# Expert weights loaded in units of 14 KB runs, one column step, two PSUM banks per token group

## The reference, cut to what matters

```python
def moe_swiglu(x, w_router, b_router, w1, w3, w2):
    logits = jnp.dot(t, w_router) + b_router                  # t: 256 x 1024
    top_val, top_idx = lax.top_k(logits, TOP_K)               # 2 of 8 experts
    top_w = jax.nn.softmax(top_val, axis=-1)
    gates = jnp.sum(jax.nn.one_hot(top_idx, N_EXPERTS) * top_w[..., None], axis=1)
    out = jnp.zeros_like(t)
    for e in range(N_EXPERTS):
        he = jax.nn.silu(t @ w1[e]) * (t @ w3[e])             # w1, w3: 1024 x 3584
        out = out + gates[:, e:e + 1] * (he @ w2[e])          # w2: 3584 x 1024
```

## Time and profile before

| | |
|---|---|
| median of 3 runs | 1250.5 us (1250.17 to 1252.01) |
| the profiled execution | 1252.75 us, span 1250.9 us |
| mean granted TensorE clock | 0.995 |
| busy: TensorE, its weight loads, VectorE, ScalarE, GpSimd | 1159.9, 664.2, 324.1, 261.7, 89.8 us |
| DMA | 114,767 packets, 421.65 MB, mean 337 GB/s; 98,256 packets under 8 KB |

### The profile page before, as it was taken

How to read it: one execution, slowest core, us unless ns; L and a number is a source line. 1 busy time by engine, 2 the same in 40 slices (tenths; PEclk the granted TensorE clock), 3 DMA queues, 4 the chain that set the end, 5 groups by cost and what they waited for, 6 DMA issues and landing times.

```text
span 1250.9 us, 28459 instructions
## 1 busy us (share of the span) xinstructions
PE 1159.9 (93%) x12516; PEld 664.2 (53%) x12517; DVE 324.1 (26%) x542; ACT 261.7 (21%) x394; POOL 89.8 (7%) x131
## 2 busy tenths in 40 slices
PE   8999999999999999999999877899987789998874
PEld 7888888888985346344346323334622332453232
DVE  6977766667974000000000000000000000000000
ACT  5885344335851000000000000000000000000000
POOL 4402200000001000100000100000010000001000
PEclk9999999999999999999999999999999999999998
DMA  7559565561498999999999999999999999999994
GB/s 237 191 178 323 190 199 183 187 202 68 153 364 319 362 373 419 405 399 409 421 404 410 407 405 410 410 421 400 409 407 404 404 409 418 399 404 409 419 401 150
DMA packets 114767, 421.65 MB, mean 337 GB/s; under 512 B 8722, under 2 KB 45199, under 8 KB 98256
## 3 DMA queue, kind: packets, MB, share of 16 engines
q1 hardware_dynamic: 109680, 413.18, 84.6%
q0 software_dynamic: 4960, 6.61, 2.2%
HBM read 416.54 MB, written 4.72 MB: 337 GB/s over the span
## 4 chain that ended last, share of the span: by engine, by line
PE 69%; DMA 23%; SPq 3%; DVE 2%; ACT 1%; issue 1%; POOL 0%; POOLq 0%; ACTq 0%; DVEq 0%
PE ps L1279 27%; PE ps L1304 13%; DMA w_raw<-in_moe_w_dram 11%; DMA w_hi_raw<-in_moe_w_dram 11%; PE ps L1010 7%; PE ps L727 5%; PE ps L729 5%; PE ps L728 5%; PE ps L1015 3%; SPq L544 3%; PE ps L1266 1%; DMA residual<-in_x_dram 0%; PE ps L1241 0%; PE ps L848 0%; PE ps L1257 0%
## 5 line engine op out<-in xcount | busy, mean ns | idle before, releaser
L1279 PE MATMUL ps<-w_raw,expert_in 128*32 128x512 f32 (+1 forms) x3416 | 342.1, 540 | 26.3 <-DMA w_raw<-in_moe_w_dram 25.3
L1279 PEld LDWEIGHTS ps<-w_raw,expert_in 128*32 128x32 f32 x3416 | 107.1, 110 | 244.3 <-issue 173.4
L1304 PE MATMUL ps<-w_raw,expert_hT 128*32 128x256 f32 x3040 | 174.1, 380 | 16.4 <-DMA w_raw<-in_moe_w_dram 16.4
L2333 DVE TENSOR_TENSOR expert_h<-expert_h,ps 128x1536 f32<-128x1536 f32 (+3 forms) x16 | 21.1, 1321 | 605.1 <-PE ps L1279 605.1
L1279 PE MATMUL ps<-w_hi_raw,expert_in 128*32 128x512 f32 (+1 forms) x1488 | 155.5, 548 | 13.9 <-DMA w_hi_raw<-in_moe_w_dram 13.9
L1304 PEld LDWEIGHTS ps<-w_raw,expert_hT 128*32 128x32 f32 x3040 | 95.8, 110 | 90.2 <-DMA w_raw<-in_moe_w_dram 24.0
L1770 DVE TENSOR_TENSOR w_lo<-w_raw,w_hi 128x2048 fp32r<-128x2048 f32 (+2 forms) x63 | 127.5, 2050 | 35.5 <-ACT w_hi L1346 35.4
L1010 PE MATMUL ps<-act_both,w_hi 128*128 128x512 f32 x352 | 122.4, 396 | 0.0
L1279 PEld LDWEIGHTS ps<-w_hi_raw,expert_in 128*32 128x32 f32 x1488 | 47.3, 111 | 111.0 <-issue 76.6
L1346 ACT ACTIVATE w_hi<-w_raw 128x2048 fp32r<-128x2048 f32 (+2 forms) x62 | 104.4, 1717 | 3.7 <-DMA w_raw<-in_mla_w_kvb_dram 2.1
L1015 PE MATMUL ps<-act_both,w_lo 128*128 128x256 f32 x352 | 91.3, 280 | 0.0
(11 more groups left out here) (365 smaller groups left out, 1105.7 us busy)
## 6 DMA issues: line engine op xcount, KB each, us to landing
w_raw<-in_moe_w_dram SPq DMA_DIRECT2D x160, 1024.0 KB, 18.9
w_hi_raw<-in_moe_w_dram SPq DMA_DIRECT2D x69, 1024.0 KB, 18.4
w_raw<-in_moe_w_dram SPq DMA_DIRECT2D x86, 768.0 KB, 22.8
w_raw<-in_ffn_w_dram SPq DMA_DIRECT2D x33, 1024.0 KB, 5.7
w_hi_raw<-in_moe_w_dram SPq DMA_DIRECT2D x36, 768.0 KB, 23.3
w_res_raw<-in_moe_w_dram SPq DMA_DIRECT2D x11, 1024.0 KB
w_raw<-in_lru_w_in_dram SPq DMA_DIRECT2D x8, 1024.0 KB, 5.4
w_res_raw<-in_moe_w_dram SPq DMA_DIRECT2D x6, 768.0 KB
```

Of the source, the lines that this page charges most:

```text
L1279: ins = pe.matmul(ps[j * STRIP:(j + 1) * STRIP, bank + g, 0:part], in_x[:, c, k, g * STRIP:(g + 1) * STRIP], w[:, j * part:(j + 1) * part] ...
L1304: ins = pe.matmul(ps[j * STRIP:(j + 1) * STRIP, bank, at:at + part], hT[t][:, a:a + STRIP], w[:, k * D + j * part:k * D + (j + 1) * part], ...
L2333: dve.tensor_tensor(h, h, regions(3, many, part), ALU.mult).then_inc(h_ready, 1)
```

## The change

- A unit of w1 or w3 is now 128 whole rows: 128 runs of 3584 columns, 14 KB. A unit of w2 is half of seven rows for each partition: a strip of 896 rows is seen as 128 partitions x 7 rows, and a unit holds the first or the second 3.5 rows of each, 14 KB in one run (28 KB apart). An expert has 24 units (8, 8, 8) in place of 46.
- The ring has 11 places of 14 KB across the raw and hi slots (each spans two or three of them). A place is free for the first load when all slots under it are (`place_free`). The place over the residual is gone; `expert_h` and `expert_out` lie there now, and the first silu waits for the residual's store.
- There is one column step. A quarter is 896 columns, more than a bank holds, so a token group has two banks (512 and 384 columns), six for three groups. w3 goes into the banks that w1 had, so its first unit waits for each group's silu. Silu, product, transposes and copy are made per group.
- The transposes read `expert_h` with a step of 7 elements, so that their rows fit the new order of w2's rows. In the middle one of the seven rows two strips take their columns from the first unit, two from the second.
- The first slot pick of expert 0 stands behind the fourth unit of w1, the next expert's between w1 and w3; VectorE takes the slots before its first product. `turn_in` uses banks 4 and 5 and stands behind the third of w2's four strips.

```diff
+    PART = EFF // STRIPS
+    PIECES = ((0, BANK), (BANK, PART - BANK))
+    RUN = PART // P
+    MID_ROW = RUN // 2
+    HALF_RUN = RUN * D // 2
+    N_BODY = 2 * KD + DOWNS
+    RING = RAW_SLOTS * UNIT // EFF + HI_SLOTS * UNIT // EFF
...
+    def place_free(i):
+        return max(free_at[cell] for cell in range(i * EFF // UNIT, ((i + 1) * EFF - 1) // UNIT + 1))
+    ring_place = sorted(range(RING), key=place_free)
...
-                for u, (name, k0, nk, c0, w) in enumerate(body_units):
-                    src = {"w1": w1, "w3": w3, "w2": w2}[name][:, k0 * P:(k0 + nk) * P, c0:c0 + w]
-                    if isinstance(n, int) and base + u < RING:
-                        sp.wait_ge(unit_used, ring_free[u])
-                        if ring_home[u][0] == "res":
-                            sp.wait_ge(rx_turned, 2 * TT)
-                            sp.wait_ge(out_sem, 16 * TT)
+                for u in range(N_BODY):
+                    if u < 2 * KD:
+                        w, k = (w1, w3)[u // KD], u % KD
+                        src = w[:, k * P:(k + 1) * P, :].rearrange("o p n -> p o n")
+                    else:
+                        strip, half = (u - M_W2) // 2, (u - M_W2) % 2
+                        src = w2[:, strip * PART:(strip + 1) * PART, :].rearrange("o (p r) n -> p o (r n)", p=P)
+                        src = src[:, :, half * HALF_RUN:(half + 1) * HALF_RUN]
...
+                def up(first_unit):
+                    for k in range(KD):
+                        w = landed(first_unit + k)
+                        for g in range(many):
+                            if first_unit == M_W3 and k == 0:
+                                pe.wait_ge(silu_ready, g_base + (g + 1))
+                            for b, (at, wide) in enumerate(PIECES):
+                                for j in range(STRIPS):
+                                    ins = pe.matmul(ps[j * STRIP:(j + 1) * STRIP, 2 * g + b, 0:wide],
+                                                    in_x[:, c, k, g * STRIP:(g + 1) * STRIP],
+                                                    w[:, j * PART + at:j * PART + at + wide],
+                                                    start=k == 0, stop=k == KD - 1, tile_position=(0, j * STRIP))
+                        if static and n == 0 and first_unit == M_W1 and k == MID_ROW:
+                            pick_slots(0, 0, 0)
+                def turn(g):
+                    pe.wait_ge(h_ready, g_base + (g + 1))
+                    for b in range(RUN):
+                        ins = pe.transpose(ps[:, 2 * g + b // 4, b % 4 * P:(b % 4 + 1) * P],
+                                           e_h[:, g * PART + b:g * PART + b + (P - 1) * RUN + 1:RUN], ident[:])
...
-                up(M_W1, 0, 0)
-                up(M_W3, 0, 3)
+                up(M_W1)
+                if static and n + 1 < E:
+                    pick_slots(n + 1, (n + 1) % 2, n + 1)
+                up(M_W3)
+                for g in range(many):
+                    turn(g)
+                down()
...
+                def silu(g):
+                    strips_past(act, u_base + (past(M_W1 + KD - 2, many) + g + 1))
+                    if static and n == 0 and g == 0:
+                        act.wait_ge(out_sem, 16 * TT)
+                    act.activation(e_h[:, g * PART:(g + 1) * PART], group_sums(g), ACT.Silu).then_inc(silu_ready, 1)
...
-                for t in range(MSTEPS):
-                    mult(t)
-                    if t == 0 and static:
-                        if n == 0:
-                            take_slots(0, 0, 0)
-                        if n + 1 < E:
-                            take_slots(n + 1, (n + 1) % 2, n)
+                if static:
+                    if n == 0:
+                        take_slots(0, 0, 0)
+                    if n + 1 < E:
+                        take_slots(n + 1, (n + 1) % 2, n)
+                for g in range(many):
+                    mult(g)
```

More of the change, by code:

```diff
@@ L461, in held, with past, used_before, first @@
             return value if isinstance(value, int) else engine.snap(value)
[L463 removed]
+        def past(u, many):
+            return u + 1 + (many - 1) * ((u >= KD - 1) + (u >= 2 * KD - 1))
+        def used_before(n):
+            def first(n):
+                return n * past(N_BODY - 1, GROUPS) - 2 * sum(GROUPS - g for g in groups[0:n])
+            return first(n) if isinstance(n, int) and n <= E else n * past(N_BODY - 1, GROUPS) - 2 * sum(GROUPS - g for g in groups)
+        def strips_past(engine, count):
             for j in range(STRIPS):
[L466 to L469 removed]
+                engine.wait_ge(strip_used[j], count)
+        def group_sums(g):
+            return ps[:, 2 * g:2 * g + 2, :].rearrange("p b n -> p (b n)")[:, 0:PART]
         def landing(n, u):
```

223 lines of the change are left out of this document (90 added, 133 removed).

## The result

| | before | after |
|---|---|---|
| median of the runs, us | 1251.26 (1250.17 to 1252.86) | 1235.36 (1234.59 to 1237.19) |
| profiled execution: span, own time, us | 1250.9, 1252.75 | 1233.7, 1235.46 |
| first matmul of expert 0, of expert 1, on the last unit, us | 389.35, 506.51, 1237.45 | 386.04, 499.65, 1218.54 |

The ratio is 0.9871 (0.9859 to 0.9883): 15.9 us faster. The forecast was 1228.8, 21.7 us faster; the range of 1218 to 1240, which took in rivals 1 to 3, holds the result, and the forecast's own range of 1224 to 1234 does not. A second measurement of the changed kernel on another chip gave 1236.44 and 0.9879 (0.9856 to 0.9902).

A forecast was written before the change was run, and what follows sets the result against it. The prediction took weight loading, paid per run, as the bound from the end of expert 0. Terms -18.5 - 3.4 - 1.5 + 1.7 = -21.7 took 1250.5 to 1228.8 us; range 1218 to 1240, the forecast's own 1224 to 1234.

The forecast's parts named there:

- rivals 1 to 3: Length stops paying at 8 KB (1238.8 us, chance 0.11), loading gains more (1219.8, 0.10), strided transposes (1236.8, 0.07).
- What bounds: Expert stage: loading is the bound from the end of expert 0 to the last landing, and pays per run.
- Run length: Expert weight loads: 14 KB runs save 2.8 us per expert over 6.6 experts, -18.5 us.
- Expert 0: TensorE at the slot picks: 1.8 us idle and 1.6 us at a lower clock both go, -3.4 us.
- The ring: Weight ring in expert 0: loading ends it one unit behind instead of 9.4 us behind, -1.5 us (0 to -3).
- The tail: Work on the last unit after it lands: twice as much as the 1.93 us before, +1.7 us.
- Other traffic: From expert 1's start to the last unit: 35 us of other traffic and a not yet empty queue, left unchanged.
- Strided transposes: Transposes reading expert_h with a step of 7 elements cost 4 times as much in expert 0, +8: 1236.8 us; chance 0.07.
- length stops paying at 8 KB: Weight loads: no gain beyond 8 KB, 4.34 us a unit, run length gives only -8.5: 1238.8 us; chance 0.11.
- Long packets dearer: Every weight load: long packets cost more per byte, priced at 565 ns each, 1266.7 us; chance 0.06.
- cut pieces: Weight loads: DMA engines cut a 14 KB row into the same pieces as before, 1258 us; chance 0.03.
- Loading gains more: w2's 4 KB runs were dearer and other traffic shrinks: run length -26, ring -3, 1219.8 us; chance 0.10.

The follow-up runs named there:

- run 9: Changed kernel with expert 0's first slot pick put back behind the product with w1, slots still taken before the first product: 1237.12 us.
- run 6: Changed kernel with a ring of 10 units instead of 11, the eleventh's memory unused: 1241.4 us, ratio 0.9921 to the kernel before.
- run 7: Changed kernel with the 20 scattered additions replaced by a GpSimd memset without any transfer, experts' output share left out: 1226.34 us.
- run 8: Kernel before with the 20 scattered additions replaced by a GpSimd instruction without any transfer, experts' output share left out: 1242.25 us.
- run 11: Changed kernel with the seven token gathers replaced by a GpSimd memset without transfer, right tokens left out from expert 1 on: 1224.27 us.
- run 12: Kernel before with no token gathers from expert 1 on, a memset in their place, right tokens left out: 1241.19 us.

## Why the prediction was right, and where it was not

**What bounds.** Right: loading sets the time from expert 1 on, and it pays per run. The line through three sizes held at 14, 7 and 3.5 KB (4.285, 4.36 and 4.5 us a unit).

**Run length, forecast -18.5.** By cadence it is 2.65 us an expert (before: 105.49, after: 102.84), times 6.6: **-17.5 us**. The mechanism was right and nearly the size: the forecast had 2.8 us an expert.

**Expert 0, forecast -3.4.** Measured 117.16 - 113.61 = **-3.55 us**. The step "the first pick stands behind the fourth unit and VectorE takes the slots before any product: both losses go" names two things and does not divide the gain; run 9 shows that the first alone is worth about 1 us. That the forecast is met to 0.2 us is in part luck: of its two losses the wait (1.8 us) is in every trace of the old stage, the clock (1.6 us) is nothing in one of them and 3 us in another. That the end sees it all was not tested: in run 9, 0.8 us in expert 0 are 0.2 to 0.6 on the last unit.

**The ring, forecast -1.5.** Measured **+1.3 us**. By the packets started until expert 1's first matmul, the queue had moved 61.7 MB of the experts' weights before and 61.2 after, of 352.3; less the 44.0 of expert 0, that is 17.7 and 17.1 MB ahead, out of rings of 20.1 and 20.2. The step that failed is "loading ends it one unit behind instead of 9.4 us behind". The 9.4 us are no measure of arrears: in the changed kernel the two loads issued in 480:490, where the queue has time to spare, also take 9.4 us from issue to landing. The ring was nearly full in both kernels, so there was little to catch up. That the larger unit keeps its place until all of it is used, 1.8 MB against 1.0, may be why the lead is a little less; it was not tested. What a place is worth was priced rightly (4.3 us forecast, 5 to 6 measured in run 6); the change gives none.

**The tail, forecast +1.7.** From the start on the last unit to the end 15.16 us, before 13.45: **+1.7**.

**Other traffic, "I leave these as they are".** This is the largest miss. From expert 1's first matmul to that on the last unit lie 718.9 us; 6.611 experts of 102.84 are 679.9, so 39.0 us are not explained by run length (38.7 in the second trace). Before: 730.9 less 6.599 of 105.49, or 696.1, leaves 34.8. So **+4.2 us**, and its cause stays open between two.

The other queue: by the medians of runs 7, 8, 11 and 12 its additions cost both kernels the same and its gathers 1 us more in the changed one, within 3 to 4 us. Their traces lean the other way. The same sum leaves 28.4 against 26.6 us without additions and 26.8 against 25.5 without gathers, so that the +4.2 shrink to +1.8 and +1.3. Each of the four is one execution.

The engines' spread: 22 us at the end against 11, and the mean engine 9.6 us ahead of the slowest against 6.7. That would be 2.9 us which the 16 engines together had the time to move but the slowest did not; over all traces it is 1.9. The spread grows with the run in all these kernels: by the same reading of the packets it is 9 us with runs of 3.5 KB, 10 to 13 with 4 to 8 KB, 17 with 7 KB, and 18 to 22 with 14 KB, whether additions or gathers are there or not. Why one engine lags was not tested, nor was a version that evens them out; that the spread costs time is argued from the windows.

**Together:** -17.5 + 1.3 + 4.2 - 3.55 + 1.7 = -13.9 us from the first matmul of expert 0 to the end. The spans differ by 17.2, because that first matmul comes 3.3 us sooner, for which the prediction has no term. Most of this is scatter: in four traces with the old expert stage it stands between 387.1 and 389.4, in ten with the new one between 386.0 and 387.9. About 1 us may be real. The medians differ by 15.9, so 1 us is left over, less than two executions of one kernel can differ by.

The packets under 8 KB went down by 47,872 (98,256 to 50,384), where the prediction had 45,056: it did not count the 16 packets of 4 bytes that each of the 176 transfers less had for its count.

**The rivals.** *Strided transposes* (1236.8) comes nearest in time, and *length stops paying at 8 KB* (1238.8) next, nearer than the forecast; both are wrong in mechanism. The second wanted 4.34 us a unit, the first some 400 ns more for each transpose: it is 14 ns, 0.3 us in expert 0. The Trainium skill ("SBUF — State Buffer", section "Door 1: The DMA port swizzle") has a step beyond 16 bytes pay for each access, without saying how much; here a step of 28 bytes cost 292 ns a transpose where adjacent elements cost 278, the same in all ten and all four traces. If those 14 ns are its price, it is small for this read. *Long packets dearer* and *cut pieces* are refuted by the 4.285 us. *Loading gains more*: no two starts that waited for loads, one unit apart, are less than 4.26 us apart.

## What to carry to other kernels

When loading bounds a kernel, take the time of one run at each length that the trace has, fit a fixed part and a slope, and read the gain from the line; here it held over a factor of four in length. Then look at the last 20 us of the loads: if the rate decays while units still land at the full distance, the engines have drifted apart, and the sum has to be made for the slowest as well as for the mean. Before a stall is credited to an instruction's place, see what else stood on the engine that it waited for: here the wait belonged to a long product on VectorE more than to the pick's own place. And before a fall of the clock is priced from one trace, look at others of the same code: here the same wait went with three different clocks.

## What the hardware showed that I had not expected

- Three plain transfers of 64 bytes from one partition to device memory, written as 4-byte packets, held the weights at 160 in place of 422 GB/s for 6 us; over the kernel they cost 1.2 us each, more than twice a scattered addition of up to 128 rows of 1 KB (0.45 us).
- The 16 engines end up to 22 us apart after 700 us of loading, and nearly twice as far with 14 KB runs (18 to 22 us) as with 4 to 8 KB runs (10 to 13).
- Around the same wait of 1.8 us on the same work, TensorE's granted clock over 430:440 was 0.83, 0.66, 1.00 and 0.83 in four executions.
- The other queue's additions land later beside long runs, at no cost to the end that runs 7 and 8 could show. DMA issues in 500:1200 of the changed kernel, then with 7 KB runs (count, median us from issue to landing); before, the median was 9.7:

```profile
out_dram<-expert_out,slot_row POOLq DMA_INDIRECT x18, 14.1
fetched_rows<-normed_tokens,slot_token POOLq DMA_INDIRECT x6, 10.7
```

```profile
out_dram<-expert_out,slot_row POOLq DMA_INDIRECT x18, 9.4
```
